# A fused attention and pooling block: the V stage taken k by k, pass 1 of the output product taken by column halves, and the last head's squares summed by VectorE

## The chip, the core and the metric

The kernel runs on one core of one Trainium2 chip. The metric is the device time in microseconds (us). Smaller is better. TensorE (PE) does matrix products into eight PSUM banks, VectorE (DVE) and ScalarE (ACT) do elementwise work, GpSimd (POOL) and SyncE (SP) issue most of the transfers. Each engine works through its own instruction list in order and is held up only by semaphores.

## The reference

`h = rms_norm(x, norm_w)` for 512 rows of 2048, then `proj = h @ w_in` with 6144 columns, split into q, k, v, an attention gate, a pooling input u and a pooling gate.

```
q, k = rope(rms_norm(q)), rope(rms_norm(k))            # per head of 64, two components c
a    = softmax(q0 k0^T / 8) - lam * softmax(q1 k1^T / 8)
attn = rms_norm(a @ v, subln_w) * 0.8                  # 8 heads, 128 wide
pool = (centred_mean(u, w) - u) @ w_pool * pool_scale  # windows 2, 4, 8, 16
out  = x + concat(attn * silu(g_a), pool * silu(g_p)) @ w_out
```

Everything is float32. In the kernel each float32 operand is split into a high and a low part (`w_hi`, `w_lo`, `h_hi`, `h_lo`), and each product is three products: high by high, low by high, high by low.

## The kernel before

**Weights** arrive from HBM in 512 KB pieces ("units") in four slots of `raw`, each unit holding two *halves* of 128 x 512. For each half ACT copies the high part into `w_hi` (four slots) and DVE writes the rest into `w_lo` (L952, `split_rest`). ACT may fill a slot when PE has released it (`w_used`), four halves back, so ACT and DVE run about three halves ahead of PE.

**V stage** (`v_half`, 32 halves of 12 products): half `v` is column half `b` = v // 16 and contraction tile `k` = v % 16. Banks 0 to 3 collect b = 0 and banks 4 to 7 collect b = 1. All of x (transposed, `x_turned`) is therefore wanted during the first 16 halves. ACT makes `h_hi` and DVE `h_lo` of each k, and banks are emptied into `v_all` by `v_high` (ACT, L727) and `v_low` (DVE, L970): those of b = 0 between halves 17 and 20, those of b = 1 during the K stage that follows (8 halves of 12 products, banks 0 and 1).

**Four rounds** (`pe_round`, `act_round`, `dve_round`), one for each pair of heads. A loop counter `m` from 8 to 47 orders the work; at each m PE does one half of a projection and, at some m, attention products. In the last round m = 40 to 47 is instead pass 0 of the output product, two *output halves* (`out_half`) each.

**Head normalisation.** After `head_done` ACT squares the head's output (m = 39 and 44), the squares are summed over 128 partitions, ACT makes `(mean + eps) ** -0.5` by a logarithm and an exponential, DVE scales the head and multiplies by the gate (`head_mixed`). The sum is made by DVE in `fold_head` (a transpose, a reduction and eight small operations), except for the second head of the last round. There the squares are split into `hsq_hi` and `hsq_lo` and PE multiplies them with a matrix of ones (two products at m = 45), `log_exp` works on 128 x 512 numbers in PSUM.

**Output product.** It is done as seven passes over 1024 x 1024 quadrants of `w_out` and sums of them, 16 output halves each; the half `h` = 16 p + hj belongs to pass p and has 6 products. A pass has a weight tile for each j = 0 to 7 (`w_tile(p, j)`, 128 x 1024, 512 KB), two column parts (`part`) each. `BY_PART` names the passes that go through all eight j for part 0 and then through all eight for part 1; the others take part 0 and part 1 of each j in turn. Passes 1, 2, 4 and 6 use one set of eight tiles: j = 0 to 3 in the slots of `raw`, j = 4 to 7 in `wide_b`. The tiles of pass 1 are loaded by SP (`load_wide`, L338): j = 0 to 3 as the slots come free during pass 0, j = 4 to 7 after its last `w_lo`. For pass 2 POOL adds another quadrant of `w_out` onto each tile in place by an accumulating DMA (`add_wide(1, j, 0, 1)`, L482), issued when DVE has finished with both parts of that tile. POOL goes on in the same way for passes 4, 5 (`tall`, L491) and 6, 32 adds in all. `tall` (passes 3 and 5) is loaded by SP, one 512 KB tile each time that an add for pass 2 has landed (L439).

Before an output half of pass 0 or of part 0, PE waits for the low part of the mixed activations of its pair of j (`form_lo_ready`). The last pair of pass 1 needs the last head. PE's other waits at this place are `rstd_ready` before half 16 (the bank of the sum with ones) and `head_normed` before half 17, because pass 1 writes the banks in which the heads stood.

```
def p_halves(p, j, part):
    return IN_HALVES + P_HALVES * p + (part * KP + j if p in BY_PART else 2 * j + part) + 1

def add_wide(p, j, row, col):
    pool.wait_ge(w_lo_ready, p_halves(p, j, 1))
    pool.dma_start(w_tile(p, j), w_block(row, col, j), accum_op=ALU.add).then_inc(wide_added[j], 16)
```

Of the kernel before, what the change touches and what calls it, by code (L numbers as in the profile page):

```python
# [23 lines left out]
def hybrid_block(nc, x, x_cols, norm_w, w_in, q_norm_w, k_norm_w, lq1, lk1, lq2, lk2, subln_w, w_pool,  # L24
# [33 lines left out]
    V_COLUMN, POOL_BANK = 2 * A, 2  # L58

    with ExitStack() as ctx:  # L60
# [46 lines left out]
        hsq_hi, hsq_lo = kh_twice[:, 1, 0], q_stack[:, 0, 1]  # L107
# [24 lines left out]
        ones_all_r = sb("ones_all_r", [P, P], F32R)  # L132
# [40 lines left out]
        BY_PART = (0, PASSES - 1)  # L173
# [53 lines left out]
        x_in = [sem(f"x_in{i}") for i in range(6)]  # L227
# [29 lines left out]
        last_squared, last_low_ready, last_summed = sem("last_squared"), sem("last_low_ready"), sem("last_summed")  # L257
# [57 lines left out]
        def _(sp):  # L315
            def load_x_cols(n, a, b):
                sp.dma_start(x_turned[:, a:b, :], x_col_tiles[:, a:b, :]).then_inc(x_in[n], 16)
# [35 lines left out]
            load_x_cols(3, 4, 8)  # L353
            load_v(2)
            load_v(3)
            load_x_cols(4, 8, 12)

            for u in range(UNITS):
# [8 lines left out]
                if u == 0:  # L367
                    load_x_cols(5, 12, 16)
                if u == 1:
# [9 lines left out]
                if 2 <= u < 2 + ST:  # L379
                    load_x_row(u - 2)  # L380
# [115 lines left out]
        def _(pe):  # L496
# [18 lines left out]
            def v_half(v):  # L515
                b, k = divmod(v, KT)
# [59 lines left out]
            def pe_round(r, last_round=False):  # L576
                for m in range(8, 8 + HALVES):
                    g, hk = divmod(m - 8, G_HALVES)

                    if hk == 0 and g == Q:  # L580
                        pe.wait_ge(pool_mixed, r * 2 + START)
                    if hk == 0 and g == U:
                        pe.wait_ge(qk_normed, r + 1)
# [19 lines left out]
                    if 0 <= i < ITEMS and not odd:  # L603
# [4 lines left out]
                        if i == 0:  # L608
                            pe.wait_ge(k_moved, r * 64 + 64)
                            if r == 0:  # L610
                                pe.wait_ge(v_lo_ready, 2 * ST)
                            else:
                                pe.wait_ge(exp_done, r * (2 * ITEMS))
# [43 lines left out]
            pe.wait_ge(v_lo_ready, ST)  # L657
# [13 lines left out]
        def _(act):  # L671
# [6 lines left out]
            def x_high(q, parts=(0, 1)):  # L678
                if q:
                    act.wait_ge(x_in[2 if q == 1 else 2 + q // 2], 16)  # L680
                for kk in parts:
                    k = 2 * q + kk
                    if q == 0:
                        act.wait_ge(x_in[kk], 16)
                    nc.scalar.activation(h_hi[:, k, :], x_turned[:, k, :], ACT.Copy,
                                         scale=nw[:, k:k + 1]).then_inc(h_hi_ready, 1)
# [36 lines left out]
            def v_high(t, b):  # L723

                act.wait_ge(x_rstd_ready, 1)
                act.wait_ge(w_used, (b + 1) * KT)
# [48 lines left out]
            def act_round(r, last_round=False):  # L775
                for m in range(8, 8 + HALVES):
# [79 lines left out]
                    if m in (39, 44):  # L856
# [5 lines left out]
                        if last_round and h:  # L862
                            for to in (head_outs[h][:, :], hsq_hi):
                                nc.scalar.activation(to, ps[:, HEAD_BANK[h], :], ACT.Square).then_inc(last_squared, 1)
                        else:
# [3 lines left out]
                    if last_round and m == 46:  # L869

                        act.wait_ge(last_summed, 1)
                        log_exp(head_outs[1][:, :], ps[:, 1, :], 2 * HEAD_DIM, eps_t[:, :], r * 3 + 3)
                    if m in ((43,) if last_round else (42, 46)):
# [13 lines left out]
            split_first(0)  # L887
            act.wait_ge(nw_in, 16)
            x_high(0, (1,))
            split_first(1)  # L890
# [3 lines left out]
            for n in range(1, HALVES):  # L894
                if n % 2 and n <= 11:
# [7 lines left out]
                if KT < n <= KT + ST:  # L903
                    v_high(n - KT - 1, 0)
                if 2 * KT < n <= 2 * KT + ST:
                    v_high(n - 2 * KT - 1, 1)
# [19 lines left out]
        def _(dve):  # L926
# [12 lines left out]
            def x_low(q, parts=(0, 1)):  # L939
                for kk in parts:  # L940
                    k = 2 * q + kk
# [481 lines left out]
```

## Time and profile before

| what | us |
|---|---|
| median of 3 runs | 750.26 (750.2 to 750.78) |
| the profiled execution's own time | 750.0 |
| its span, first to last instruction | 748.2 |
| PE busy | 742.9 (99% of the span) |
| DVE busy | 572.7 (77%) |
| ACT busy | 378.7 (51%) |
| POOL busy | 34.7 (5%) |
| 16 DMA engines, 612 to 700 us of the span | busy share 1.02 to 1.06 |

The span is what the trace covers, and 1.8 us of the execution lie around it. A busy share above 1 of the DMA engines means that packets overlap; they have no gaps. The granted clock of TensorE was 1.00 of the full 2.4 GHz in every stretch.

### The profile page before, as it was taken

To read this page: it belongs to the slowest core of one execution; us is meant where nothing else is said; L and a number is where in the kernel's file an instruction comes from. 1 tells how busy PE (TensorE), PEld (TensorE's weight loads), DVE (VectorE), ACT (ScalarE), POOL (GpSimd) and SP (SyncE) were. 2 spreads that over 40 slices of the span, in tenths; PEclk is the share of its full clock that TensorE was granted. 3 is DMA by queue.
4 is the path that set the end of the run, shared out by engine and by line. 5 is a ranking of instruction groups with operands and counts; after the bars stand their busy time and mean duration, and the time that the engine had idled before them with its cause. 6 is when DMAs were issued, how large, how long until landed. Compare 5 with 4: busy or idle time off the path is not lost.

```text
span 748.2 us, 9167 instructions
## 1 busy us (share of the span) xinstructions
PE 742.9 (99%) x3268; PEld 613.5 (82%) x3268; DVE 572.7 (77%) x986; ACT 378.7 (51%) x665; POOL 34.7 (5%) x47
## 2 busy tenths in 40 slices
PE   9999999999999999999999999999999999999997
PEld 7888888888888888888888888888888888888886
DVE  5543247898785898885889888588988988987895
ACT  5472232456563255664344576224566776555552
POOL 0020000000000000000000000000000003312200
PEclk9999999999999999999999999999999999999999
DMA  8873333434432343433234444144344659999972
GB/s 317 294 270 102 95 89 120 125 117 124 117 112 60 124 141 111 125 105 110 73 121 130 124 123 120 57 127 128 112 120 120 182 177 270 276 276 260 211 178 111
DMA packets 84842, 111.39 MB, mean 149 GB/s; under 512 B 7360, under 2 KB 64960, under 8 KB 84288
## 3 DMA queue, kind: packets, MB, share of 16 engines
q1 hardware_dynamic: 78496, 92.85, 39.8%
q0 software_dynamic: 4864, 16.78, 11.3%
q10 hardware_dynamic: 1440, 1.19, 0.5%
q8 instruction: 26, 0.43, 0.2%
q14 instruction: 16, 0.13, 0.1%
HBM read 94.03 MB, written 4.19 MB: 131 GB/s over the span
## 4 chain that ended last, share of the span: by engine, by line
PE 99%; DMA 0%; DVE 0%; issue 0%; SPq 0%; DVEq 0%
PE ps L504 99%; DMA mixed<-in_x_cols 0%; DVE x_left L1371 0%; SPq L347 0%; DVE h_hi L1224 0%; DVEq L60 0%; DVEq L1221 0%
## 5 line engine op out<-in xcount | busy, mean ns | idle before, releaser
L504 PE MATMUL ps<-h_lo,w_hi 128*128 128x512 f32 x640 | 249.1, 389 | 0.0
L504 PE MATMUL ps<-h_hi,w_hi 128*128 128x512 f32 x640 | 249.1, 389 | 0.0
L952 DVE TENSOR_TENSOR w_lo<-raw,w_hi 128x512 fp32r<-128x512 f32 x240 | 163.0, 684 | 100.6 <-ACT w_hi L710 53.6
L504 PE MATMUL ps<-h_hi,w_lo 128*128 128x512 f32 x640 | 171.1, 389 | 0.0
L720 ACT CAST w_hi<-raw 128x512 fp32r<-128x512 f32 x149 | 92.1, 621 | 131.4 <-PE ps L504 131.2
L504 PEld LDWEIGHTS ps<-h_lo,w_hi 128*128 128x128 f32 x640 | 120.1, 188 | 25.2
L504 PEld LDWEIGHTS ps<-h_hi,w_hi 128*128 128x128 f32 x640 | 120.1, 188 | 25.1
L504 PEld LDWEIGHTS ps<-h_hi,w_lo 128*128 128x128 f32 x640 | 120.1, 188 | 24.9
L504 PE MATMUL ps<-w_hi,h_hi 128*128 128x512 f32 x352 | 121.6, 390 | 0.3 <-DVE h_hi L1224 0.2
L504 PE MATMUL ps<-w_hi,h_lo 128*128 128x512 f32 x352 | 121.4, 389 | 0.0
L504 PE MATMUL ps<-w_lo,h_hi 128*128 128x512 f32 x352 | 121.4, 389 | 0.0
L504 PEld LDWEIGHTS ps<-w_hi,h_hi 128*128 128x128 f32 x352 | 65.9, 188 | 14.6 <-issue 0.9
L504 PEld LDWEIGHTS ps<-w_hi,h_lo 128*128 128x128 f32 x352 | 66.0, 188 | 14.0 <-DVE h_lo L946 0.2
L504 PEld LDWEIGHTS ps<-w_lo,h_hi 128*128 128x128 f32 x352 | 66.1, 188 | 13.7
L816 ACT ACTIVATE probs<-ps,neg_scaled,q_rstd 128x512 f32<-128x512 f32 x64 | 49.2, 774 | 36.9 <-DVE neg_scaled L1119 36.9
L710 ACT CAST w_hi<-raw 128x512 fp32r<-128x512 f32 x43 | 26.2, 620 | 55.2 <-PE ps L504 45.6
L1117 DVE TENSOR_REDUCE neg_max<-ps 128x2 f32<-128x1024 f32 x32 | 39.1, 1223 | 8.9 <-PE ps L504 8.7
L773 ACT CAST w_hi<-raw 128x512 fp32r<-128x512 f32 x48 | 29.4, 622 | 21.8 <-PE ps L504 21.8
L482 POOL DMA_DIRECT2D raw<-in_w_out x12 | 10.5, 878 | 575.5 <-DVE w_lo L952 573.9
L773 ACT CAST w_hi<-tall 128x512 fp32r<-128x512 f32 x32 | 19.9, 623 | 19.4 <-PE ps L504 19.4
L773 ACT CAST w_hi<-wide_b 128x512 fp32r<-128x512 f32 x32 | 19.9, 623 | 18.9 <-PE ps L504 18.9
L1136 DVE SCALAR_TENSOR_TENSOR at_raw<-probs,coef 128x512 f32<-128x512 f32 x32 | 24.1, 752 | 5.1 <-PE ps L504 3.9
(168 smaller groups left out, 736.1 us busy)
## 6 DMA issues: line engine op xcount, KB each, us to landing
raw<-in_w_in SPq DMA_DIRECT2D x95, 512.0 KB, 3.7
at_raw<-turned SPq DMA_DIRECT2D x128, 64.0 KB, 2.1
raw<-in_w_out SPq DMA_DIRECT2D x12, 512.0 KB, 3.9
raw<-in_w_out POOLq DMA_DIRECT2D x12, 512.0 KB, 17.1
wide_b<-in_w_out POOLq DMA_DIRECT2D x12, 512.0 KB, 19.4
x_rows<-in_x SPq DMA_DIRECT2D x4, 1024.0 KB, 13.9
tall<-in_w_out SPq DMA_DIRECT2D x8, 512.0 KB, 13.1
tall<-in_w_out POOLq DMA_DIRECT2D x8, 512.0 KB, 23.4
```

Of the source, the lines that this page charges most:

```text
L482: pool.dma_start(w_tile(p, j), w_block(row, col, j), accum_op=ALU.add).then_inc(wide_added[j], 16)
L504: last = nc.tensor.matmul(dst, lhs, rhs, start=first and i == 0, stop=final and i == len(pairs) - 1, skip_group_check=True)
L710: nc.scalar.copy(w_hi[:, n % W_SLOTS, :], raw[:, unit % RAW_SLOTS, part * 512:part * 512 + 512]).then_inc(w_hi_ready, 1)
L720: nc.scalar.copy(w_hi[:, m % W_SLOTS, :], raw[:, unit % RAW_SLOTS, part * 512:part * 512 + 512]).then_inc(w_hi_ready, 1)
L773: nc.scalar.copy(w_hi[:, h % W_SLOTS, :], src).then_inc(w_hi_ready, 1)
L816: nc.scalar.activation(probs[:, c, :], ps[:, S0 + c, :], ACT.Exp, bias=neg_scaled[:, c:c + 1], scale=q_rstd[:, h, t, c:c + 1], accum_out=r ...
L952: nc.vector.tensor_tensor(w_lo[:, slot, :], src, w_hi[:, slot, :].bitcast(F32), ALU.subtract).then_inc(w_lo_ready, 1)
L1117: chain(nc.vector.reduce_max(neg_max[:, :], ps[:, S0:S0 + 2, :], AX_X, negate=True))
L1136: nc.vector.scalar_tensor_tensor(out=at_raw[:, item_place(i)[1], :], in0=probs[:, 1, :], scalar=coef[:, :], in1=probs[:, 0, :], op0=ALU.mu ...
```

## The change

1. **Last head.** The two products with ones, `ones_all_r`, `hsq_hi`, `hsq_lo`, the second square and three semaphores go. DVE calls `fold_head(1)` at m = 45, ACT calls `log_exp` on `h_sums` at m = 46, DVE also transposes the second head's factor at m = 47.
2. **Pass 1 by column halves.** `BY_PART` becomes (0, 1, 6). PE waits for `evacuated` instead of `rstd_ready` before half 16, and for `head_normed` before half 24 instead of 17.
3. **V stage k by k.** `k, b = divmod(v, 2)`. A unit of V is now one k with both column halves (4 KB in one piece per partition). x arrives in smaller groups, the first tile in two pieces with a semaphore each; its later groups, the constants and the rows of x are issued later. All V banks are emptied from n = 31 on, and PE waits for the low parts of the first two before the K stage.

```diff
-        BY_PART = (0, PASSES - 1)
+        BY_PART = (0, 1, PASSES - 1)
...
+    X_GROUPS = ((1, 2), (2, 4), (4, 6), (6, 8), (8, 12), (12, 16))
...
             def load_v(u):
-                b, kp = divmod(u, KP)
-                sp.dma_start(raw[:, u % RAW_SLOTS, :].rearrange("p (k n) -> p k n", k=2),
-                             w_in_rows[:, 2 * kp:2 * kp + 2, V_COLUMN + b * NC:V_COLUMN + (b + 1) * NC]
+                sp.dma_start(raw[:, u % RAW_SLOTS, :], w_in_rows[:, u, V_COLUMN:V_COLUMN + 2 * NC]
                              ).then_inc(raw_in[u % RAW_SLOTS], 16)
...
             sp.dma_start(raw[:, 0, 0:512], w_in_rows[:, 0, V_COLUMN:V_COLUMN + NC]).then_inc(first_half_in, 16)
-            load_x_cols(0, 0, 1)
-            load_x_cols(1, 1, 2)
-            sp.dma_start(raw[:, 0, 512:1024], w_in_rows[:, 1, V_COLUMN:V_COLUMN + NC]).then_inc(raw_in[0], 16)
-            load_x_cols(2, 2, 4)
+            for piece in range(2):
+                cols = slice(piece * (SEQ // 2), (piece + 1) * (SEQ // 2))
+                sp.dma_start(x_turned[:, 0, cols], x_col_tiles[:, 0, cols]).then_inc(x_first[piece], 16)
+            sp.dma_start(raw[:, 0, 512:1024], w_in_rows[:, 0, V_COLUMN + NC:V_COLUMN + 2 * NC]).then_inc(raw_in[0], 16)
+            load_x_cols(0)
             load_v(1)
...
-                if 2 <= u < 2 + ST:
-                    load_x_row(u - 2)
+                if 6 <= u < 6 + ST:
+                    load_x_row(u - 6)
...
             def v_half(v):
-                b, k = divmod(v, KT)
+                k, b = divmod(v, 2)
...
-                    if last_round and m == 45:
-
-                        pe.wait_ge(evacuated, ROUNDS * 3 + START)
-                        pe.wait_ge(last_low_ready, 1)
-                        products(ps[:, 1, :], [(ones_all_r[:, :], hsq_hi), (ones_all_r[:, :], hsq_lo)],
-                                 True, True).then_inc(last_summed, 1)
...
-            pe.wait_ge(v_lo_ready, ST)
+            pe.wait_ge(v_lo_ready, 2)
...
-            pe.wait_ge(rstd_ready, ROUNDS * 3 + START)
+            pe.wait_ge(evacuated, ROUNDS * 3 + START)
             for h in range(P_HALVES, PASSES * P_HALVES):
-                if h == P_HALVES + 1:
+                if h == P_HALVES + KP:
                     pe.wait_ge(head_normed, ROUNDS * 2 + START)
...
-                        if last_round and h:
-                            for to in (head_outs[h][:, :], hsq_hi):
-                                nc.scalar.activation(to, ps[:, HEAD_BANK[h], :], ACT.Square).then_inc(last_squared, 1)
-                        else:
-                            squares(head_outs[h][:, :], ps[:, HEAD_BANK[h], :])
+                        squares(head_outs[h][:, :], ps[:, HEAD_BANK[h], :])
...
+                if V_HALVES - 1 <= n < V_HALVES + 3:
+                    b, pair = divmod(n - V_HALVES + 1, 2)
+                    v_high(2 * pair, b)
+                    v_high(2 * pair + 1, b)
                 split_first(n + 3)
-                if 11 <= n <= 14:
-                    x_stats(n - 11)
...
+                if 17 <= n <= 20:
+                    x_stats(n - 17)
...
-                    if last_round and m == 45:
-
-                        dve.wait_ge(last_squared, 2)
-                        nc.vector.tensor_tensor(hsq_lo, head_outs[1][:, :], hsq_hi.bitcast(F32), ALU.subtract
-                                                ).then_inc(last_low_ready, 1)
...
-                        if not last_round or h == 0:
-                            chain(nc.vector.transpose(head, repeated(h_rstd[:, :])))
+                        chain(nc.vector.transpose(head, repeated(h_rstd[:, :])))
...
-                    if last_round and m == 42:
-                        fold_head(0)
+                    if last_round and m in (42, 45):
+                        fold_head(int(m == 45))
...
-                if n == 15:
+                if n == 21:
                     dve.wait_ge(x_squared, ST)
...
-                if n == 27:
+                if n == 30:
                     dve.wait_ge(eps_spread, 1)
```

## Rows read from the trace of the kernel before

**Rows 1.** The chain that ended last, in order of time: start, us, what.

```profile
5.12 3.05 PE ps L504 x12
...
8.29 735.89 PE ps L504 x3238
```

**Rows 2.** Timeline, first 10 us: start, duration, engine and line, operation, count [idle before].

```profile
0.98 3.94 PE L499 MATMUL ps<-gate 128*128 128x128 f32 x18 [0.98 <-POOL gate L467]
...
7.53 0.62 ACT L710 CAST w_hi<-raw 128x512 fp32r<-128x512 f32 x1 [0.96 <-DMA raw<-in_w_in]
```

**Rows 3.** Timeline of ACT and DVE where a V bank is emptied.

```profile
96.20 0.68 ACT L727 ACTIVATE v_all<-ps,x_rstd 128x512 fp32r<-128x512 f32 x1
...
96.94 0.75 DVE L970 SCALAR_TENSOR_TENSOR v_all<-ps,x_rstd,v_all 128x512 fp32r<-128x512 f32 x1
```

**Rows 4.** Timeline of POOL in the V stage.

```profile
50.48 2.36 POOL L470 DMA_DIRECT2D probs<-x_eps  x4 [49.55 <-DVE x_eps L1251]
...
58.37 1.23 POOL L477 PARTITION_BROADCAST rstd_row<-gate  x1 [2.45 <-DMA gate<-x_rstd]
```

**Rows 5.** Timeline of PE at the end of pass 0: the first product with ones, the first of half 16.

```profile
607.51 0.39 PE L504 MATMUL ps<-kh_twice,ones_all_r 128*128 128x512 f32 x1
...
613.45 0.39 PE L504 MATMUL ps<-w_hi,h_hi 128*128 128x512 f32 x1
```

**Rows 6.** Timeline of DVE in the last round.

```profile
596.10 0.71 DVE L1023 STREAM_TRANSPOSE h_turned<-head_out 128x512 f32<-128x512 f32 x1
...
598.99 0.17 DVE L1030 TENSOR_TENSOR h_sums<-h_half,h_shift 128x16 f32<-128x16 f32 x1
...
604.99 0.68 DVE L1144 TENSOR_TENSOR q_stack<-eps_row,kh_twice 128x512 fp32r<-128x512 f32 x1
...
610.06 1.29 DVE L952 TENSOR_TENSOR w_lo<-raw,w_hi 128x512 fp32r<-128x512 f32 x2 [1.38 <-ACT w_hi L773]
```

**Rows 7.** Timeline of SP's transfers: the tiles of pass 1.

```profile
601.01 10.10 SPq L338 DMA_DIRECT2D raw<-in_w_out  x4
611.15 2.17 SPq L338 DMA_DIRECT2D wide_b<-in_w_out  x4
```

**Rows 8.** One tile's instructions on SP: the four tiles j = 4 to 7 of pass 1.

```profile
L338 SPq DMA_DIRECT2D wide_b<-in_w_out x4: 432/481/645, 611.2 to 612.7; - x4
...
DMA to landing us min/median/max: 6.5/8.5/12.9
```

**Rows 9.** Timeline of ACT: first splits of pass 2, its tile 7, pass 6's tile 7.

```profile
631.38 0.62 ACT L773 CAST w_hi<-raw 128x512 fp32r<-128x512 f32 x1 [0.79 <-PE ps L504]
...
650.42 0.62 ACT L773 CAST w_hi<-wide_b 128x512 fp32r<-128x512 f32 x1 [0.27 <-PE ps L504]
...
727.94 0.62 ACT L773 CAST w_hi<-wide_b 128x512 fp32r<-128x512 f32 x1 [0.74 <-PE ps L504]
```

**Rows 10.** One tile's instructions on POOL: adds 1, 8 and 32.

```profile
L482 POOL DMA_DIRECT2D raw<-in_w_out x1: 929/929/929, 613.7 to 613.7; - x1
...
DMA to landing us min/median/max: 9.6/9.6/9.6
...
L482 POOL DMA_DIRECT2D wide_b<-in_w_out x1: 866/866/866, 631.7 to 631.7; - x1
...
DMA to landing us min/median/max: 17.7/17.7/17.7
...
L482 POOL DMA_DIRECT2D wide_b<-in_w_out x1: 863/863/863, 706.1 to 706.1; - x1
...
DMA to landing us min/median/max: 19.7/19.7/19.7
```

**Rows 11.** DMA queues in 612 to 618, 640 to 655 and 688 to 700 us: packets, MB, share.

```profile
q1 hardware_dynamic: 458, 1.69, 92.8%
...
q0 software_dynamic: 562, 2.06, 68.6%
...
q0 software_dynamic: 697, 2.54, 106.7%
```

More of the change, by code:

```diff
@@ L226, in hybrid_block @@
         nw_in, ones_set = sem("nw_in"), sem("ones_set")
-        x_in = [sem(f"x_in{i}") for i in range(6)]
+        x_first = [sem(f"x_first{i}") for i in range(2)]
+        x_in = [sem(f"x_in{i}") for i in range(len(X_GROUPS))]
         first_half_in = sem("first_half_in")
@@ L315, in _, with load_x_cols @@
         def _(sp):
-            def load_x_cols(n, a, b):
+            def load_x_cols(n):
+                a, b = X_GROUPS[n]
                 sp.dma_start(x_turned[:, a:b, :], x_col_tiles[:, a:b, :]).then_inc(x_in[n], 16)
@@ L366, in _ @@
                     load_in(Q, nxt - UNITS, 0)
-                if u == 0:
-                    load_x_cols(5, 12, 16)
-                if u == 1:
+                if u in (0, 2, 4):
+                    load_x_cols(3 + u // 2)
+                if u == 3:
                     for dst, src in ((cos_t[:, :], rope_cos),
@@ L581, in pe_round @@
                         pe.wait_ge(pool_mixed, r * 2 + START)
+                        if r == 0:
+                            pe.wait_ge(v_lo_ready, 2 * ST)
                     if hk == 0 and g == U:
@@ L676, in _, with x_high @@
             act.wait_ge(setup_step, 1)
[L678 to L686, printed above, removed]
+            def x_high(k):
+                for n, (first, end) in enumerate(X_GROUPS):
+                    if k == first:
+                        act.wait_ge(x_in[n], 16)
+                nc.scalar.activation(h_hi[:, k, :], x_turned[:, k, :], ACT.Copy,
+                                     scale=nw[:, k:k + 1]).then_inc(h_hi_ready, 1)
             def x_stats(t):
@@ L861, in act_round @@
                         act.wait_ge(scored, r * ITEMS + ITEMS)
-                        if last_round and h:
-                            for to in (head_outs[h][:, :], hsq_hi):
-                                nc.scalar.activation(to, ps[:, HEAD_BANK[h], :], ACT.Square).then_inc(last_squared, 1)
-                        else:
-                            squares(head_outs[h][:, :], ps[:, HEAD_BANK[h], :])
+                        squares(head_outs[h][:, :], ps[:, HEAD_BANK[h], :])
                     if last_round and 43 <= m < 46:
                         form_high(1, m - 43)
[L869 to L873, printed above, removed]
+                    if m in ((43, 46) if last_round else (42, 46)):
                         h = int(m == 46)
@@ L894, in _ @@
             for n in range(1, HALVES):
-                if n % 2 and n <= 11:
+                if n % 2 and n <= 27:
                     x_high((n + 3) // 2)
@@ L937, in _, with x_low @@
                 dve.sem_inc(started, START)
-            def x_low(q, parts=(0, 1)):
-                for kk in parts:
-                    k = 2 * q + kk
-                    if k:
-                        dve.wait_ge(h_hi_ready, k)
-                    else:
-                        dve.wait_ge(first_h_ready, 2)
-                    nc.vector.scalar_tensor_tensor(
-                        out=h_lo[:, k, :], in0=x_turned[:, k, :], scalar=nw[:, k:k + 1],
-                        in1=h_hi[:, k, :].bitcast(F32), op0=ALU.mult, op1=ALU.subtract).then_inc(h_lo_ready, 1)
+            def x_low(k):
+                if k:
+                    dve.wait_ge(h_hi_ready, k)
+                else:
+                    dve.wait_ge(first_h_ready, 2)
+                nc.vector.scalar_tensor_tensor(
+                    out=h_lo[:, k, :], in0=x_turned[:, k, :], scalar=nw[:, k:k + 1],
+                    in1=h_hi[:, k, :].bitcast(F32), op0=ALU.mult, op1=ALU.subtract).then_inc(h_lo_ready, 1)
             def split_rest(slot, src, count):
@@ L1233, in _ @@
             for n in range(1, HALVES):
-                if n % 2 and n <= 11:
+                if n % 2 and n <= 27:
                     x_low((n + 3) // 2)
@@ L1268, in _ @@
                     setup(nc.vector.memset(q_shift[:, :, :], 0.0))
+                if V_HALVES - 1 <= n < V_HALVES + 3:
+                    b, pair = divmod(n - V_HALVES + 1, 2)
+                    v_low(2 * pair, b)
+                    v_low(2 * pair + 1, b)
                 split_rest((n + 3) % W_SLOTS, raw_half(n + 3), n + 4)
-                if KT < n <= KT + ST:
-                    v_low(n - KT - 1, 0)
-                if 2 * KT < n <= 2 * KT + ST:
-                    v_low(n - 2 * KT - 1, 1)
-            setup(nc.vector.memset(ones_all_r[:, :].bitcast(F32), 1.0))
             for r in range(ROUNDS - 1):
```

24 lines of the change are left out of this document (7 added, 17 removed).

## The prediction

> **What bounds the kernel now.** I read the page first: PE is busy for 99% of the span and the chain that ended last is PE almost throughout. In order of time the chain has 12 products from 5.12 us in 3.05 us, then 3238 products in one unbroken piece of 735.89 us [rows 1]. That is 0.2273 us each and no stall at all, so every microsecond in which PE is kept waiting after 8.29 us is added to the end, and the only time to be won is in removed products and in the first half. 12 products take 2.72 us, an output half (6) 1.36 us. The profiled execution took 750.0 us, 0.26 below the median of the runs; its span is 748.2 and 1.8 lie around it.
>
> What can make PE wait must then be read from distances: how long before its use does each input stand ready? ACT fills a slot as soon as PE begins the third half before the one that uses it: it split tile 0 of pass 2 (half 32) at 631.38 [rows 9], and half 32 started at 613.45 + 16 x 1.36 = 635.21 [rows 5], 3.83 us later. Less 0.62 on ACT and 0.75 on DVE with its semaphore, 2.46 us are spare before PE stalls. So data late for ACT by less than 2.46 us cost nothing, and what exceeds that is paid in full. I looked for the edges at which this change shortens such a distance.
>
> **The change part by part.**
>
> *First half.* PE's warm-up products end at 4.92 us (0.98 + 3.94) [rows 2], and the first real ones start at 5.12. They begin no sooner than 4.92, so the smaller first piece of x can give 0.2 at most. The 12 products of half 0 then take 8.29 - 5.12 = 3.17 instead of 2.72 us, because the split of half 1 starts only at 7.53, when its weights land as the fourth 256 KB piece [rows 2]. Now they come third, with x's second tile behind them. I take 0.1 to 0.2 of the first and all 0.45 of the second: **-0.55** (bounds: 0, if the new order lands no earlier, and -0.65).
>
> *Removed products.* Two at 0.2273: **-0.45**.
>
> *Rest of the V stage.* A k now feeds two halves, so each 5.44 us want 256 KB of x and 512 KB of weights instead of 256 and 256 in 2.72: less, and x no longer starves. When half 30 ends, ACT empties two banks at 0.68 each and DVE follows with 0.75 [rows 3]; ACT's next starts about 0.6 after the first. Two low parts are ready about 0.1 + 0.6 + 0.68 + 0.06 + 0.75 = 2.2 us later, half 31 lasts 2.72. Hidden with 0.5 us to spare, cost 0; without that cover it would be at most the 2.2. POOL's spreading of eps and rstd takes from 50.48 to 59.60 = 9.1 us [rows 4], and has n = 21 to 30, nine halves or 24.5 us. The rows of x are issued at n = 13, 15, 17, 19 and read seven to four halves later (19 to 11 us); a late one falls on an ACT with nothing else to do and three halves of lead. All zero.
>
> *Last head.* PE's sum goes, but DVE, which is the fuller engine here, gets a `fold_head` of 596.10 to 599.16 = 3.06 us and a transpose of about 0.7, and loses one subtraction of 0.68 [rows 6]. Worked through in order: split 12, `form_low` and split 13 follow from 604.99 at 0.6 apart and end by 606.9, the fold by 609.9, split 14 to 610.45. Half 14 would start at 613.45 - 2.72 - 0.45 = 610.28 [rows 5]: a stall of **0.25**. The low part of half 15 stands at about 611.75, against 610.06 + 0.69 = 610.75 before [rows 6]. In m = 47 the transpose, the norm and the gate (0.7 + 0.75 + 0.7) stand ahead of split 17, whose low part ends at 615.2, for a half due at 614.6: **0.7** with semaphores. Together +0.95 (bounds 0 and 2.4, the whole net DVE work less 0.7).
>
> *Pass 1's own tiles.* SP's load of tile 3 and its wide loads wait for the low part of half 15; wide loads began at 611.15 [rows 7], and now about 1.0 later. They landed 6.5 us after issue for tile 4 and 12.9 for tile 7, with POOL's adds among them [rows 8]. Before, tile 4 was wanted at hj = 8; now it is wanted at hj = 4, 5.4 us sooner, and tile 7 at hj = 7 instead of 14, 9.5 us sooner. Tile 4: landed 612.1 + 6.5 = 618.7, low part ready 1.4 to 1.5 later, 620.2, for a half which with the stalls so far starts at 619.4: +0.9. The hardware queue alone moved 1.69 MB in 6 us [rows 11], so a tile takes 1.86 us. Tiles 5, 6, 7 land at about 620, 621.8, 623.5 for halves each 1.36 apart: +0.6 more. Together **+1.5** (bounds 0, if SP is not delayed, and 4).
>
> *The adds for pass 2.* This is the main term. Add j may be issued after the low part of part 1 of tile j. That was hj = 2j + 1, and is hj = 8 + j. Add 1 was issued at 613.7 and landed 9.6 us later; add 8, issued at 631.7, landed at 631.7 + 17.7 = 649.4 [rows 10]. Pass 2 wanted tile 0 at 631.38 and tile 7 at 650.42 [rows 9]: the spare fell from 8.1 to 1.0 us, since adds land one in (649.4 - 623.3) / 7 = 3.74 us while pass 2 eats one in 2.72. The pace is a limit of the transfers: with both queues busy the software queue moved 2.06 MB in 15 us, 3.8 us for 512 KB, and alone 2.54 MB in 12 us, 2.5 us [rows 11]. Its first packets came more than 4 us after the first issue: no packet of it stands among those of 612 to 618 [rows 10, 11]. Now:
> - Half 24 starts at 613.45 + 8 x 1.36 - 0.45 + 0.95 + 1.5 = 626.3. After a stall the splits are just ahead of PE, so the low part of half 24 is ready at 626.0 and the first add is issued at 626.3, 12.6 us later than before.
> - It moves alone: 4.65 to the first packet, 2.5, 0.45 to the semaphore: lands at 633.9 (bound above: 9.6, so 635.9). The second follows 2.5 behind, at 636.4, and then `tall`, which SP sends as each add lands, shares the engines and the pace is 3.75: add 8 lands at 636.4 + 6 x 3.75 = 658.9.
> - Half 46, the first of tile 7, can start 1.5 later, 660.4. Without this wait it would start at 626.3 + 22 x 1.36 = 656.3: **+4.1** (bounds 0 and 7.4).
>
> *Later passes.* The software queue stays behind: add 32 landed at 706.1 + 19.7 = 725.8 [rows 10], and pass 6 wanted it at 727.94 [rows 9]. The queue's start is 12.6 later, of which 2.0 and 0.8 come back in the first two adds, which run alone: 735.7. Wanted: 727.94 + 6.15 = 734.1, plus the spare (here 1.5, DVE is behind): **+0.1** (bounds 0 and 1.5). Tiles in `tall` keep over 5 us.
>
> Sum: -0.55 - 0.45 + 0.95 + 1.5 + 4.1 + 0.1 = +5.65. 750.0 + 5.65 = 755.65, and with the 0.26 of the median about **755.9**.
>
> The trace's 4.65 us from issue to first packet and 9.6 to landing [rows 10, 11] stand against the Trainium skill, "DMA: Bandwidth & Descriptors", section "Anatomy of one DMA — SWDGE (gpsimd) path", which fits a software-queue transfer as 2.0 us plus bytes over 436e3, so 3.2 us for 512 KB. By it the first add lands at 629.5 and add 8 at 654.5, the term of 4.1 vanishes and the sum is about 751.9; the trace does not agree.
>
> **The rivals.**
> - *The adds catch up* (the second stall doesn't come): an add issued into empty engines lands within about 5 us, not 7.6, and the pace is nearer 2.5 than 3.75 while SP's tiles are still on their way. For it: no add of before ran into empty engines. Against: 3.74 and 3.8 in two views. Then +1.6, 751.7. The same number comes if only the late adds bite and the first stalls don't: first add issued at 621.9, add 8 at 654.5, half 46 at 656.0 instead of 654.3, so +1.7 - 0.55, 751.4. 0.17.
> - *No wait appears, and it is faster:* the spares hold. This decides at add 8 landing before 652.3 (650.42, less 0.45, plus 2.46 less semaphores), which needs first landings by about 627, issue plus 5. Then -1.0: 749.3. 0.09.
> - *DVE never catches up:* the fold, the late tiles and pass 2's own sums on DVE add up, and the first add also lands in 9.6: about 760 and above. Against: DVE idles while it waits for late tiles. 0.06.
> - *Later V banks stall the K stage:* by the 0.5 us of cover at most a few tenths. It changes no sum.
>
> **How the numbers follow.** Both stalls, 752 to 760, has 0.68, and 755.9 is its centre. With one of them 0.17, none 0.09, worse 0.06. Leaving out no stall and the tail above gives the range 751.2 to 759.8. A difference under 0.2% (1.5 us) can't be told from no change here. Faster by more is the case without waits that keeps over 1.5 (few) plus luck with its 1.0: mostly it lands at -1.0, within 0.2%, so I give faster 0.06, same 0.15 (the rest of it and half of the one-stall cases), slower 0.79.
>
> **What will show it.** Half 0 in 2.7 us, half 1 started near 7.7: first term. PE's list of waits, empty before, names `w_lo` or `w_hi` behind SP's wide loads at pass 1, hj = 4 to 7 (term 5), and behind POOL's adds in pass 2, hj growing from 8 to 14 (term 6), with ACT's splits waiting for DMA. The first add's issue to landing should be 7 to 8 us, the next ones at 3.75. If PE still runs in one piece, I am wrong on the distances; if the stall sits at hj = 0 to 3 of pass 1, the head's fold is the larger term.

## The result, and the profile after

The changed kernel takes 752.84 us (median of 7 runs, 752.62 to 753.3), the kernel before beside it 750.26 (7 runs, 749.46 to 750.85). The ratio is 1.0035 [1.0026, 1.0045]: slower by 0.35%. The forecast was 755.9: right in direction and within its range, but the change moved the time by 2.6 us and not by 5.65. The profiled execution took 753.05 us, 2.9 of its span more than before (751.1 against 748.2).

From the page of the changed kernel:

```profile
span 751.1 us, 9171 instructions
...
PE 744.5 (99%) x3266; PEld 613.1 (82%) x3266; DVE 575.0 (77%) x995; ACT 376.3 (50%) x664; POOL 34.7 (5%) x47
```

The list of waits of PE's weight loads (us in total, times, longest; in before this line waits for `issue`, 0.9, and `h_lo`, 0.2, alone):

```profile
PEld ps L503 <- issue: 2.1, 4, 0.8
PEld ps L503 <- DVE w_lo L931: 2.0, 3, 1.3
...
PEld ps L503 <- DVE h_hi L1197: 0.6, 1, 0.6
PEld ps L503 <- DVE h_lo L925: 0.3, 1, 0.3
```

and its chain that ended last, in order of time (start, us, what), beside [rows 1]:

```profile
5.19 580.74 PE ps L503 x2552
...
606.98 0.64 DVE h_turned L1002
...
609.95 0.60 DVE w_lo L931
...
612.18 6.17 DMA wide_b<-in_w_out
618.37 0.63 ACT w_hi L763
...
632.85 22.79 DMA wide_b<-in_w_out
655.65 0.63 ACT w_hi L763
656.31 0.70 DVE w_lo L931
657.05 90.11 PE ps L503 x396
```

The unbroken piece of PE is gone. The chain shows the three forecast places in their order: the fold on DVE (606.98 to 609.95), a wide tile that SP issued at 612.18 and whose split came at 618.37, and POOL's last add for pass 2, issued at 632.85 and split at 655.65. From 657.05 on PE runs through again, so nothing is lost in later passes of this kernel.

To size each place I took, in the timeline of PE, the starts of its products: what exceeds the steady distance of 0.2265 us between two is stall. The one or two products behind a wait start a little late as well, by 0.08 to 0.11 each, and are counted with it, here and in all experiments. Half 1 of the V stage starts at 8.64 instead of 8.29, and from half 2 on PE is 0.26 late. Two products go: -0.45. Then 0.30 before output half 14, 0.46 at 17 and 18, 0.42 before half 20 (tile 4 of pass 1), 0.63 before half 44 and 1.18 before half 46. The sum is 0.26 - 0.45 + 2.99 = +2.8, of 2.9 in the span.

DVE in the last round and ACT at the two late transfers (timelines; beside [rows 6, 9]):

```profile
606.90 0.70 DVE L1002 STREAM_TRANSPOSE h_turned<-eps_row 128x512 f32<-128x512 f32 x1
...
609.78 0.18 DVE L1009 TENSOR_TENSOR h_sums<-h_half,h_shift 128x16 f32<-128x16 f32 x1
```

```profile
618.37 0.62 ACT L763 CAST w_hi<-wide_b 128x512 fp32r<-128x512 f32 x1 [1.81 <-DMA wide_b<-in_w_out]
...
651.65 1.14 ACT L763 CAST w_hi<-wide_b 128x512 fp32r<-128x512 f32 x2 [2.12 <-DMA wide_b<-in_w_out]
...
655.65 1.14 ACT L763 CAST w_hi<-wide_b 128x512 fp32r<-128x512 f32 x2 [2.34 <-DMA wide_b<-in_w_out]
```

The fold takes 606.90 to 609.96, 3.06 us, the price read from the other head. Before half 20 and halves 44 and 46 ACT sits idle about 2 us, and what ends the idle time is a DMA: ACT's three halves of lead (how far it works ahead of PE) are used up, and PE pays what exceeds them. Tiles 6 and 7 of pass 2 come 4.00 us apart; pass 2 eats one in 2.72.

### The profile page after: what moved, and what is told of

Its sections match the earlier page's. It is cut to its first block, busy times and chain, and to the rows that moved or that the text cites. A ratio compares the mean times of both kernels' runs of the same rounds, so it can differ in the third digit from the quotient of the medians.

```text
span 751.1 us, 9171 instructions
## 1 busy us (share of the span) xinstructions
PE 744.5 (99%) x3266; PEld 613.1 (82%) x3266; DVE 575.0 (77%) x995; ACT 376.3 (50%) x664; POOL 34.7 (5%) x47
## 3 DMA queue, kind: packets, MB, share of 16 engines
q10 hardware_dynamic: 1440, 1.19, 0.6%
## 4 chain that ended last, share of the span: by engine, by line
PE 90%; DMA 4%; DVE 4%; ACT 1%; issue 1%; POOL 0%; DVEq 0%; SPq 0%; ACTq 0%; POOLq 0%
PE ps L503 89%; DMA wide_b<-in_w_out 4%; DVE w_lo L931 1%; PE ps L498 1%; DVE h_lo L959 1%; ACT w_hi L763 1%; DVE form_sum L1252 0%; DVE x_left L1261 0%; POOL wide_b L481 0%; DVE h_shift L1008 0%; DVE h_part L1003 0%; ACT L840 0%; DVE h_turned L1002 0%; ACT gate L842 0%; ACT work L844 0%
## 5 line engine op out<-in xcount | busy, mean ns | idle before, releaser
L931 DVE TENSOR_TENSOR w_lo<-wide_b,w_hi 128x512 fp32r<-128x512 f32 x32 | 21.6, 686 | 8.7 <-ACT w_hi L763 8.5
```

The lines of the kernel that those rows point to most:

```text
L931: nc.vector.tensor_tensor(w_lo[:, slot, :], src, w_hi[:, slot, :].bitcast(F32), ALU.subtract).then_inc(w_lo_ready, 1)
```

## The experiments

Each kernel was timed against the kernel before on the same chip; medians, with the ratio and its 95% interval. They ran in three sessions on three chips, so two experiments are compared by what each differs from the kernel before beside it. The theory: each term of the sum is real but over-priced, and the adds, started after the low part of half 24, are the largest. The rivals: (A) the fold takes DVE's lead and so sets off what follows; (B) only the late start of the adds counts, whoever is late; (C) the start of the V stage or the K stage after it costs too.

**One part at a time.** `v_only` is the third part of the diff (V stage k by k, x in new pieces) on the kernel before; `head_only` the first part (no products with ones, both heads folded on DVE); `p1_only` the second:

```diff
-        BY_PART = (0, PASSES - 1)
+        BY_PART = (0, 1, PASSES - 1)
...
-                if h == P_HALVES + 1:
+                if h == P_HALVES + KP:
```

and `ones_kept` is all but the first part.

> The V stage part alone. The profile of the changed kernel has its half 1 of the V stage 0.35 us later than before, not 0.55 earlier. Theory A (the two pieces of the first x tile and the order of the first loads are what costs): +0.2 to +0.3 us against before, half 0 longer than 2.72 us because its second piece lands about 5.4 us. Theory B (the slow first products are the granted clock, which rises at another moment in each execution): within 0.3 of before in the median, and half 0 as long as the clock makes it. No stall between half 2 and the end in either.

749.77 us against 750.03: 0.9994 [0.9985, 1.0003]. No stall after the first halves. The interval reaches from -1.1 to +0.2 us: it can't tell the half us forecast for the start from nothing. Rival C falls: the start and the K stage behind it cost nothing that can be seen.

> The last head's part alone. Both theories: -0.45 for two products, and stalls of about 0.3 before output half 14 and 0.45 around 17 and 18, as in the changed kernel, so -0.2 to +0.4 us in all. No stall in passes 1 to 6, since tiles and adds keep their old spares of 1 us and more.

750.33: 1.0005 [0.9996, 1.0014]. Stalls of 0.3 before half 14 and 0.44 at 17, as forecast, less the two products; none in the passes. The part costs nothing that can be measured.

> Pass 1 by column halves alone. Theory A (the parts interact: the adds are late because ACT and DVE had lost their lead when half 24 was split): the lead is full, the first add is issued at 622.3, 2.0 us before half 24 starts instead of 0.4, add 8 lands near 653, and the stall in pass 2 is 0 to 0.4 us; total 0 to +0.5. Theory B (the late release alone makes the stall): the same 1.8 us in pass 2 as in the changed kernel, total +1.8 or more. In both the tile 4 stall of pass 1 is under 0.2.

753.23: 1.0038 [1.0024, 1.0052], a miss for the theory that the parts interact (+0.0 to +0.5). Alone it costs what the whole change costs, +3.2.

> The change with its last head's part undone (the products with ones stay). Theory A (interaction): +0.2 to +0.8 us against before, so about 2 us faster than the full change although it has two products more. Theory B (each part adds its own): 2.6 + 0.45 - 0.75 = +2.3.

752.61: 1.0032 [1.0021, 1.0042], near the +2.3 of the theory that each part adds its own. The three parts alone add up to -0.26 + 0.30 + 3.20 = +3.2, together they measure +2.6, each uncertain by 0.7 to 1.1: within that they add. Rival A falls here as the only cause, and with it my first reading of the trace: without any fold, and so without any wait in the last round, pass 2 stalls no less (1.67 in `p1_only`, 2.9 in `ones_kept`, 1.81 in the changed kernel). In the timeline of `p1_only`, ACT's splits of tile 4 of pass 1 and of tile 7 of pass 2, DVE's low part for half 24, and POOL's first add:

```profile
617.79 0.62 ACT L773 CAST w_hi<-wide_b 128x512 fp32r<-128x512 f32 x1 [1.85 <-DMA wide_b<-in_w_out]
...
654.93 1.14 ACT L773 CAST w_hi<-wide_b 128x512 fp32r<-128x512 f32 x2 [2.29 <-DMA wide_b<-in_w_out]
```

```profile
623.45 0.69 DVE L952 TENSOR_TENSOR w_lo<-raw,w_hi 128x512 fp32r<-128x512 f32 x1
```

```profile
624.44 0.93 POOL L482 DMA_DIRECT2D raw<-in_w_out  x1 [566.20 <-DVE w_lo L952]
```

Tile 4 stops PE for only 0.15 us. But ACT had been 1.85 us idle for it, so the lead of the splits is gone: the low part of half 19 is ready 1.19 us before PE starts that half, that of half 20 only 0.15. Half 24, which starts at 624.81, gets its low part 0.67 before.

**The late start alone.** `late_adds` is the kernel before with pass 1 as it was, and the adds for pass 2 held back to the same half as in the change:

```diff
-                add_wide(1, j, 0, 1)
+                pool.wait_ge(w_lo_ready, IN_HALVES + P_HALVES + KP + j + 1)
+                pool.dma_start(w_tile(1, j), w_block(0, 1, j), accum_op=ALU.add).then_inc(wide_added[j], 16)
```

> Before, with one thing changed: POOL issues add j for pass 2 only after the low part of half 24 + j, as the column-half order forces it; pass 1 keeps its order by tile pairs, so no tile is wanted earlier. Theory A (the late release costs pass 2 little by itself, because the lead of DVE at half 24 is full, 2.3 us; it is the tile 4 wait in pass 1 that eats the lead and so delays the first add): first add issued at 622.3, the eighth lands 30.7 later at 653.0, stall 0 to 0.4 us. Theory B (late release alone): +1.8.

750.77 against 750.28: 1.0008 [0.9999, 1.0017]. In the trace, of its fastest execution, PE stalls once after the start, 0.30 us at half 46 (its list of waits puts 0.5 down to that place, measured on the weight load, which runs ahead). Rival B falls too: the same release rule alone costs 0.5 in the median, and the interval ends at 1.3, far below the +3.2 of `p1_only`. Its rows say why: DVE's low part for half 24, PE's first product of that half, the first add, and where add 8 is split:

```profile
621.27 0.69 DVE L953 TENSOR_TENSOR w_lo<-wide_b,w_hi 128x512 fp32r<-128x512 f32 x1
```

```profile
624.28 0.39 PE L505 MATMUL ps<-w_hi,h_hi 128*128 128x512 f32 x1
```

```profile
622.27 0.93 POOL L486 DMA_DIRECT2D raw<-in_w_out  x1 [563.38 <-DVE w_lo L953]
```

```profile
653.00 1.14 ACT L774 CAST w_hi<-wide_b 128x512 fp32r<-128x512 f32 x2 [2.29 <-DMA wide_b<-in_w_out]
```

Here DVE is 624.28 - 621.96 = 2.3 us ahead of PE, so the half that releases the first add is split two halves early, and the add goes out 2.0 us before that half starts. In the changed kernel DVE's low part for half 24 is this one:

```profile
623.98 0.68 DVE L931 TENSOR_TENSOR w_lo<-raw,w_hi 128x512 fp32r<-128x512 f32 x1
```

It ends at 624.66 for a half that starts at 625.39: 0.7 ahead, and the add goes out 0.4 before it. The 1.6 us between them are lost lead. In `p1_only` the wait for tile 4 took them; in the changed kernel the fold had taken them already (the low part of half 17 is ready 0.05 us before its half), and the wait for tile 4 then kept the lead from coming back.

**The two together.** In pass 1 DVE starts two operations, 0.60 us apart, in each half of 1.36, and so regains only about 0.15 us per half; from half 20 to 24 that is 0.6. If that is the mechanism, removing the wait at tile 4 must give the lead back, and most of the stall in pass 2, in a kernel that has no fold. `p1_early` is `p1_only` with SP's wide loads issued sooner, `early_only` the changed kernel with the same edit, where loading of tiles 4 to 6 goes between the first ones:

```diff
-            sp.wait_ge(head_done, ROUNDS * 2)
-            for j in range(RAW_SLOTS, KP):
-                load_wide(j)
...
+                if u >= 5:
+                    sp.wait_ge(head_done, ROUNDS * 2)
+                    load_wide(u - 1)
+            load_wide(KP - 1)
```

> Pass 1 by column halves alone with the early tiles. Theory A: the tile 4 wait is gone, DVE keeps its lead, first add at 622.3, pass 2 stalls 0.0 to 0.4 us: +0.0 to +0.6 against before, 2.5 us less than pass 1 by halves without the early tiles. Theory B: pass 2 keeps 1.5 to 1.8 us.

751.2 against 750.28: 1.0015 [1.0006, 1.0024], so +0.9 where `p1_only` had +3.2, between what the two theories give. The wait for tile 4 is gone, and with it the stall before half 44:

```profile
622.77 0.93 POOL L483 DMA_DIRECT2D raw<-in_w_out  x1 [564.11 <-DVE w_lo L953]
```

```profile
PEld ps L505 <- DVE w_lo L953: 1.2, 1, 1.2
```

The add goes out 1.7 us before half 24 starts, and 1.03 of stall stays at half 46. It is 0.7 more than in `late_adds`: the add goes out 0.3 less ahead, and add 8 is split 31.2 us after the first issue and not 30.7, since the first add landed 6.4 us after issue and not 5.4.

> The full change with tiles 4 to 7 of pass 1 loaded earlier, whole adds. Both theories: the 0.4 us before half 20 go. Theory A: DVE has 1.2 us of lead at half 24 (0.7 in the full change), so the first add comes 0.5 earlier against PE and 1.2 to 1.4 us of the 1.8 us stall in pass 2 stay: about +1.7 against before. Theory B: all 1.8 stay: +2.2.

751.87: 1.002 [1.0011, 1.0029], +1.6 for a forecast of +1.7. Its profiled execution was the slowest of its eleven (754.49 us; the next took 752.59), so its stalls are not those of the median. It shows two things all the same. The wait for tile 4 is gone, but the first add goes out only 0.66 us before half 24, for 0.42 in the changed kernel: with the fold in place the lead is short even so. And the first add, issued into empty engines, landed only 7.9 us later:

```profile
L482 POOL DMA_DIRECT2D raw<-in_w_out x1: 929/929/929, 624.4 to 624.4; - x1
...
DMA to landing us min/median/max: 7.9/7.9/7.9
```

Pass 2 stalls 3.7 us there, before halves 40, 42, 44 and 46. The seven traces in which the adds for pass 2 start this late, side by side (us; "ahead" is from the issue of the first add to the start of half 24, "landing" from its issue to its landing, "split" from its issue to ACT's split of add 8):

| kernel | ahead | landing | split | stall in pass 2 |
|---|---|---|---|---|
| `late_adds` | 2.01 | 5.4 | 30.73 | 0.30 |
| `p1_early` | 1.71 | 6.4 | 31.17 | 1.03 |
| `fold_moved` | 0.55 | 5.5 | 30.24 | 1.25 |
| `p1_only` | 0.37 | 5.5 | 30.49 | 1.67 |
| the change | 0.42 | 5.7 | 30.68 | 1.81 |
| `ones_kept` | 0.42 | 6.9 | 31.76 | 2.9 |
| `early_only` | 0.66 | 7.9 | 32.88 | 3.7 |

In every row the stall is "split" less "ahead" less 28.4 or 28.5. So two things of about the same size set it: the lead, worth up to 1.6, and how long the first add takes to land, worth up to 2.5. Behind that landing the pace is alike in all seven: add 8 is split 24.7 to 25.3 us later. Between `late_adds` and `p1_only` or the change the landing is nearly the same, so there the difference is the lead.

**The fold, and the adds in halves.** `half_adds` is the changed kernel with the adds for pass 2 in two 256 KB pieces each, of which the first is released eight halves sooner:

```diff
-            for j in range(KP):
-                add_wide(1, j, 0, 1)
+            for part in range(2):
+                cols = slice(part * 512, (part + 1) * 512)
+                for j in range(KP):
+                    pool.wait_ge(w_lo_ready, p_halves(1, j, part))
+                    pool.dma_start(w_tile(1, j)[:, cols], w_block(0, 1, j)[:, cols], accum_op=ALU.add
+                                   ).then_inc(wide_added[j], 16)
```

> The full change, with each add for pass 2 made in two of 256 KB, the one of part 0 issued as soon as part 0 of the tile is split (half 16 + j), the other at 24 + j. If the late release of the adds makes the stall of pass 2, the 1.8 us there go: 751.0, +0.8 against before. If the pace of the software queue or smaller transfers cost as much, the stall stays or moves, +2 or more. The fold's 0.75 and tile 4's 0.4 stay in both, tile 4's may grow to 1 with adds beside the wide loads.

754.6 against 750.05: 1.0062 [1.0048, 1.0076], slower than the change itself. The stall in pass 2 is gone, as expected, but the adds now share the DMA engines with the wide loads of pass 1, and these are late one after the other; ACT's splits of tiles 6 and 7:

```profile
622.60 0.62 ACT L767 CAST w_hi<-wide_b 128x512 fp32r<-128x512 f32 x1 [2.00 <-DMA wide_b<-in_w_out]
...
625.16 0.62 ACT L767 CAST w_hi<-wide_b 128x512 fp32r<-128x512 f32 x1 [1.94 <-DMA wide_b<-in_w_out]
```

PE stalls 0.9, 1.3 and 1.1 at halves 20, 22 and 23. (The kernel also raises the counts that SP and ACT wait for, since each tile now has two adds.) `early_wide` is `half_adds` with the early wide loads.

> half_adds, and tiles 4 to 6 of pass 1 issued one each behind tiles 1 to 3, tile 7 behind them. Tile 4 lands by 612, so the stall of 0.4 before half 20 goes: +0.3 to +0.5 against before. If the loads queue up and tile 2 or 3 comes late instead, the stall moves to half 18 or 19 and the time stays at that of half_adds.

750.63: 1.0008 [0.9999, 1.0017]. Now both transfers are in time, and all that stays behind the start is the stall at the fold, 0.30 and 0.46 as in the change; the list of waits names it with one wait of 0.5 for `w_lo`.

```profile
PEld ps L508 <- DVE w_lo L936: 0.5, 1, 0.5
```

That closes the account: with the transfers moved apart nothing of the loss but the fold's 0.8 is left, less the 0.45 of the two products.

`fold_moved` is the changed kernel with the second head's fold cut in two, its end put behind split 14 (m = 46), and the head's norm behind split 17 (m = 47); `mended` is that order on `early_wide`:

```diff
+                    if last_round and m == 47:
+                        split_form_low(2 * m - 77)
+                    if last_round and m == 46:
+                        fold_end()
...
-                    if last_round and m in (42, 45):
-                        fold_head(int(m == 45))
+                    if last_round and m == 42:
+                        fold_head(0)
+                    if last_round and m == 45:
+                        fold_start(1)
```

> The full change, with the second half of the last head's fold put behind split 14, and the head's normalisation behind split 17. Stalls of 0.3 before half 14 and 0.45 at 17 and 18 go. Theory A (the lead that DVE loses here is what makes the adds late): most of the 1.8 in pass 2 goes too, -1.5 to -2.5 against the full change, +0.1 to +1.1 against before. Theory B (each part adds its own): -0.75 against the full change, +1.8 against before.

754.16 against 750.05: 1.0053 [1.0039, 1.0067], a miss: +4.1, 1.5 more than the change. ACT's timeline:

```profile
611.32 0.31 ACT L722 ACTIVATE h_rstd<-h_sums,eps_t 128x16 f32<-128x16 f32 x1 [4.03 <-DVE h_sums L1015]
...
616.53 0.62 ACT L746 CAST h_hi<-mixed 128x512 fp32r<-128x512 f32 x1 [2.16 <-DVE mixed L1196]
```

ACT is in order too: it stands 4.03 us at the wait for the fold, and the split for half 15 stands behind it. PE loses 1.42 there and 1.29 before half 18, where ACT waits for the gated head. Another 0.44 goes at half 68, in pass 4, and 0.20 at the same place in `p1_only`: DVE waits 1.8 and 1.5 us for rows of x (`x_right`), whose load SP issues behind the last tile of `tall`, and so behind add 8.

> early_wide with fold_moved's order. No stall after half 1 of the V stage; the two products removed stay removed: -0.2 to -0.4 against before (0.26 of the start stays lost), 749.9. If a new wait appears it is at halves 15 to 19.

752.45: 1.0032 [1.0019, 1.0044]. The same two stalls (1.43 and 1.34), none in pass 2. The misses of both are the one oversight.

`mended2` is `early_wide` with the fold's end behind split 15, ACT's logarithm behind split 16, and DVE's splits 17 and 18 ahead of the norm:

```diff
-                    if m in ((43, 46) if last_round else (42, 46)):
+                    if m in ((43, 47) if last_round else (42, 46)):
...
+                    if last_round and m == 46:
+                        split_form_low(2 * m - 77)
+                        fold_end()
+                    if last_round and m == 47:
+                        for k in (17, 18):
+                            split_form_low(k)
```

> early_wide with the last head's work on DVE spread anew: second half of the fold behind split 15, ACT's logarithm behind split 16, the normalisation behind split 18, the last activation pair split behind half 20. No engine waits ahead of a split here. Stalls of the fold go or stay under 0.3: -0.3 to +0.1 against before, 749.8 to 750.1, and no worse than early_wide's 750.6. If DVE is simply short of time between halves 14 and 20, a stall of 0.3 to 0.8 remains at half 18 to 20.

751.37 against 750.28: 1.0015 [1.0006, 1.0024]. The stalls at 14 and 17 are gone, and 1.52 stands at half 19 and 0.27 at half 21 in their place. DVE works without a pause from 614.51 to 618.06: the norm of the head, started behind split 18, and one sum stand ahead of the low part of half 19, for which PE waits.

```profile
614.51 0.70 DVE L1198 STREAM_TRANSPOSE eps_row<-h_rstd 128x512 f32<-128x512 f32 x1
...
617.38 0.68 DVE L937 TENSOR_TENSOR w_lo<-raw,w_hi 128x512 fp32r<-128x512 f32 x1
```

ACT had split that half from 615.50 on, after 1.63 us of idle time for tile 3 of pass 1, so its high part was there 1.3 us before DVE came to the low one: the tile was late but did not decide. It is the second case of the expectation, DVE short of time, at about twice the size named there. No kernel of the study is faster than the one before; `v_only` equals it.

## Why the prediction was off in size

What bounds the kernel was read rightly: distances, an edge at tile 4 of pass 1 and one at the last tiles of pass 2. The time lies in the range because the range is wide, with its lower end 4.7 us below the forecast: the term that carries most of the sum, 4.1, measured 1.8. By the steps of the sum:

*First half (-0.55, measured about 0).* In the timeline of the changed kernel, slow first products cover what the smaller piece could have won. PE's first products, then those of the old start in `p1_only` and `head_only`:

```profile
4.84 1.94 PE L503 MATMUL ps<-w_hi,h_hi 128*128 128x512 f32 x4
...
7.21 0.62 ACT L700 CAST w_hi<-raw 128x512 fp32r<-128x512 f32 x1 [2.79 <-DMA raw<-in_w_in]
...
8.64 1.07 PE L503 MATMUL ps<-w_hi,h_hi 128*128 128x512 f32 x4
```

```profile
4.97 2.04 PE L504 MATMUL ps<-w_hi,h_hi 128*128 128x512 f32 x4
...
8.70 0.85 PE L504 MATMUL ps<-w_hi,h_hi 128*128 128x512 f32 x3
```

```profile
4.99 1.16 PE L501 MATMUL ps<-w_hi,h_hi 128*128 128x512 f32 x4 [0.40 <-DVE h_hi L1201]
...
7.88 1.07 PE L501 MATMUL ps<-w_hi,h_hi 128*128 128x512 f32 x4
```

Four products take 1.94 and 2.04 us in two executions and 1.16 in the third. Nearly 0.5 us each against the steady 0.23 is what the lower of TensorE's two clock levels (1.2 against 2.4 GHz) would look like, but the granted clock in the profile's rows is 1.00 there in all three, so that it was the clock is not shown. It doesn't go by kernel: `p1_only` and `head_only` have the same start. Half 1 starts at 8.64, 8.70 and 7.88, and with the new start in `v_only` at 7.93. In `v_only` and `head_only`, where the first products are quick, new and old differ by 0.05. The weights did come earlier (split at 7.21 instead of 7.53), but half 1 did not start earlier for it: I had taken the 0.45 of [rows 2] for the split's lateness alone.

*Removed products (-0.45)* and *rest of the V stage (0)*: right; `v_only` shows no stall past its first halves.

*Last head (0.95, measured 0.76):* 0.30 and 0.46 for 0.25 and 0.7.

*Pass 1's own tiles (1.5, measured 0.4).* The wide loads started 1.03 later, as forecast, and tile 4 was issued at 612.18 and split at 618.37, for a forecast landing at 618.7, so 0.42 for 0.9. SP's loads in the timeline of its queue, and what one tile's view gives:

```profile
601.26 10.87 SPq L336 DMA_DIRECT2D raw<-in_w_out  x4
612.18 2.17 SPq L336 DMA_DIRECT2D wide_b<-in_w_out  x4
```

```profile
L336 SPq DMA_DIRECT2D wide_b<-in_w_out x4: 432/468/670, 612.2 to 613.7; - x4
...
DMA to landing us min/median/max: 6.2/7.3/8.4
```

The other 0.6 never came. Four tiles issued within 1.5 us move at the same time: issue 613.7 + 8.4 is 622.1 for the last, so they land (622.1 - 618.4) / 3 = 1.25 apart, inside the 1.36 of a half. I had put them in a row behind one another, at 620, 621.8 and 623.5; by the 1.86 that stands there they would even have been at 620.6, 622.4 and 624.3, and the term larger.

*The adds for pass 2 (4.1, measured 0.63 + 1.18 = 1.8).* This is the step that failed, in one sentence of it: "It moves alone: 4.65 to the first packet, 2.5, 0.45 to the semaphore". The 4.65 was taken for a fixed latency from 613.7 to the queue's first packets; it stands in no row, and neither does the 0.45 to the semaphore (the trace of before has the first packets 4.4 us after the issue). In before, SP's wide loads had just filled the engines, as this row of its busy times shows (PE, PEld, DVE, ACT, POOL, then clock, DMA share, GB/s):

```profile
616.00:620.00 4.00, 4.00 (x19) 3.32 (x18) 4.00 (x7) 2.36 (x5) 1.73 (x2) 1.00 1.04 329
```

In the changed kernel they were empty. POOL's first add there, the busy times around it, and the software queue's packets in 626.5 to 628 us:

```profile
L481 POOL DMA_DIRECT2D raw<-in_w_out x1: 932/932/932, 625.0 to 625.0; - x1
...
DMA to landing us min/median/max: 5.7/5.7/5.7
```

```profile
622.50:626.50 4.00, 4.00 (x19) 3.33 (x18) 4.00 (x8) 3.50 (x7) 1.26 (x2) 1.00 0.02 6
626.50:640.00 13.50, 13.50 (x61) 11.17 (x60) 12.21 (x20) 9.24 (x16) 7.48 (x9) 1.00 1.02 208
```

```profile
q0 software_dynamic: 42, 0.17, 87.9%
```

Until 626.5 the engines stand at a share of 0.02, and 1.6 us after the issue at 624.97 the packets flow. The add lands after 5.7 us, not 7.6. `late_adds` is the kernel before with nothing but the issue moved into empty engines, and there the first packets come after 1.6 us and the add lands after 5.4. So [rows 10, 11] had shown a queue and not a latency. The first packets come 1.6 us after issue in all seven traces of the table, but the landing lies between 5.4 and 7.9, and the forecast 7.6 is inside that: for the landing it is a value that this kernel did not have, not an impossible one. The pace was right: add 1 lands at 630.7 and add 8 at 655.6, 24.9 us later, for 25.0 forecast. The term then follows in full: add 8 lands 3.3 earlier than forecast (1.9 of latency, 1.3 of an earlier issue, 0.1 of pace), while half 46 would without the wait start at 625.39 + 22 x 1.36 = 655.3, 1.0 earlier than forecast, since the last head and pass 1's tiles cost 0.76 and 0.42 and not 0.95 and 1.5, while the start cost 0.26: 4.1 - 3.3 + 1.0 = 1.8. (The forecast 626.3 for half 24 leaves out the -0.55 of its own first term. The start of half 46 and the issue of the adds are both counted from it, so the term is not changed by that. The 751.7 and 751.9 that the prediction gives for the case without this term should be one number, 751.8.)

The Trainium skill, "DMA: Bandwidth & Descriptors", section "Anatomy of one DMA — SWDGE (gpsimd) path", fits a transfer of the software queue as 2.0 us plus its bytes over 436e3, an estimate of 3.2 us for 512 KB. The traces disagree with it, with 5.4 to 7.9 into empty engines; the 5.7 of the changed kernel lies about midway between it and my 7.6.

*Later passes (0.1, measured 0).* The chain has no break after 657.05. But the edge that comes first there is not the one I named, pass 6's last tile: it is half 68, behind the rows of x, where `p1_only` loses 0.20 and `fold_moved` 0.44. In the changed kernel DVE waits 1.1 us for them and PE does not.

Rival "the adds catch up" named the latency ("within about 5 us, not 7.6") but also a faster pace and no stall; only its first half came true, with 5.7.

What I had not seen is how much of the stall in pass 2 hangs on the lead. "After a stall the splits are just ahead of PE" stands in the prediction as a side remark; the experiments make it one of two causes. With the lead whole (`late_adds`) the same rule of release costs 0.30 us of stall; with the lead lost and the first add landing about as fast it costs 1.7 to 1.8, although in `p1_only` tile 4 itself stops PE for as little as 0.15. The other cause is the time that the first add takes to land.

What stays open: whether the new start is worth anything at a fixed clock (it is below what these runs can tell), and why the first add lands anywhere between 5.4 and 7.9 us after issue in kernels that are alike there. In all seven traces its first packets come 1.6 us after issue, so the difference arises behind them; with one trace for each kernel it can't be said whether it goes with the kernel or with the execution.

## What to carry to other kernels

A wait that hardly stops the bounding engine can still use up the lead of the engines that feed it, and every release counted from their work is then late by the lead that was lost; look at how much they regain per step before you call such a wait small. A latency read where other traffic fills the engines holds queueing, so look at the DMA share of that window before it goes into a sum. And read the stalls of a slow execution too: here it is the trace that shows the second cause most clearly. Moving a transfer sooner pays only where it does not push another that is itself close to its use: the half-size adds cured one stall and made three, until the other loads were moved as well.

## What the runs showed of the hardware

- An accumulating transfer of 512 KB on the software queue into idle DMA engines landed 5.4 to 7.9 us after issue in seven traces, its first packets 1.6 us after issue in each; behind the wide loads of SP in before it was 9.6 [rows 10], with the first packets after 4.4.
- Four 512 KB loads issued within 1.5 us by one queue landed 1.25 us apart after 6.2 us: they share the engines.
- The moment at which TensorE goes from nearly 0.5 to 0.23 us per product in the first 10 us differs between executions of kernels with the same start (four products in 2.04 us in `p1_only`, in 1.16 in `head_only`); half 1 began at 8.70 and at 7.88. The granted clock reads 1.00 there in both, and no run shows the cause.
- DVE operations on two inputs of 128x512 last 0.68 us each in the timeline but start 0.60 us apart when they follow one another without a pause (623.38, 623.98 and 624.58 in the changed kernel).
